# A Trainium2 decoder layer: multiplications to GpSimd, a quarter of the copies and the query casts to VectorE, value products in runs of four pairs

## The reference, cut to what matters

```
s = q k^T * scale, masked;  m = max(s);  p = exp(s - m);  o = (p v) / sum(p)
A: 6 banded heads, window 128, a learned sink per head in the maximum and the sum
B: 6 dilated heads, (window, dilation) = (128, 1), (512, 4), (2048, 16); the three
   results are combined with weights proportional to their sums
C: 4 memory heads, every token against 256 memory tokens
y = (o_A, o_B, o_C) * silu(gate)
```

## Time and profile before

| | before |
|---|---|
| median of 3 runs | 2163.92 us (2161.46 to 2164.92) |
| the profiled execution: its span | 2163.3 us |
| its own time | its span; nothing is shown around it |
| TensorE busy | 2054.7 us (95%) |
| VectorE busy | 1557.3 us (72%) |
| ScalarE busy | 1351.1 us (62%) |
| GpSimd busy | 114.9 us (5%) |
| mean granted clock of TensorE | 0.973 |

### The profile page before, as it was taken

The page is one execution under the profiler, slowest core; times in us unless marked ns, Lnnn a source line. Parts: engine busy times, 40 slices in busy tenths (PEclk is TensorE's granted clock), DMA queues, the critical chain, the costliest instruction groups (busy, mean ns, idle before and its releaser), DMA issues. The chain is left out here.

```text
span 2163.3 us, 39340 instructions
## 1 busy us (share of the span) xinstructions
PE 2054.7 (95%) x12892; PEld 1717.7 (79%) x12892; DVE 1557.3 (72%) x4410; ACT 1351.1 (62%) x3520; POOL 114.9 (5%) x116
## 2 busy tenths in 40 slices
PE   5999899999999999999899999999899998999998
PEld 4787678888888888888777887888778887788886
DVE  6564674546664574446588989989799997888887
ACT  6454454544555464343699979989689998533333
POOL 1232310000000000002000000000000000000000
PEclk7999999999999999999799989989999999999999
DMA  4477576777577657589778676686869996245543
GB/s 157 144 243 217 170 240 179 221 242 218 154 225 223 219 182 244 199 276 273 179 147 157 133 142 135 131 166 121 166 149 214 232 270 179 98 158 175 174 158 113
DMA packets 351737, 401.40 MB, mean 186 GB/s; under 512 B 105617, under 2 KB 255249, under 8 KB 346689
## 3 DMA queue, kind: packets, MB, share of 16 engines
q1 hardware_dynamic: 343120, 364.80, 61.5%
q0 software_dynamic: 8432, 34.30, 5.1%
...
## 5 line engine op out<-in xcount | busy, mean ns | idle before, releaser
L854 PE MATMUL p_ps<-p_u_hi,p_w_hi 128*128 128x512 f32 x1344 | 534.7, 398 | 25.8 <-DVE p_p_c L739 10.6
L856 PE MATMUL p_ps<-p_u_hi,p_w_lo 128*128 128x512 f32 x1344 | 526.8, 392 | 0.0
L855 PE MATMUL p_ps<-p_u_lo,p_w_hi 128*128 128x512 f32 x1344 | 526.2, 392 | 0.0
L570 DVE TENSOR_TENSOR p_w_lo<-p_w_raw,p_w_hi 128x512 fp32r<-128x512 f32 x336 | 245.7, 732 | 331.4 <-ACT p_w_hi L423 329.8
L1621 ACT ACTIVATE probs<-probs,a_stat 128x256 f32<-128x256 f32 (+1 forms) x896 | 433.7, 489 | 49.2 <-DVE a_stat L1455 45.8
L423 ACT ACTIVATE p_w_hi<-p_w_raw 128x512 fp32r<-128x512 f32 x336 | 210.7, 628 | 331.7 <-PE p_ps L856 303.7
L854 PEld LDWEIGHTS p_ps<-p_u_hi,p_w_hi 128*128 128x128 f32 x1344 | 254.1, 189 | 86.1 <-DVE p_u_lo L577 12.0
L856 PEld LDWEIGHTS p_ps<-p_u_hi,p_w_lo 128*128 128x128 f32 x1344 | 254.0, 189 | 54.5
L1455 DVE CUSTOM_DVE_ANT_0 probs<-a_ps_s,fixed 128x256 f32<-128x256 f32 (+1 forms) x704 | 251.6, 396 | 63.2 <-PE a_ps_s L1354 61.9
L855 PEld LDWEIGHTS p_ps<-p_u_lo,p_w_hi 128*128 128x128 f32 x1344 | 254.4, 189 | 50.7
L1408 PE MATMUL a_ps_o<-a_pT,a_v 128*64 128x128 f32 x3320 | 256.7, 285 | 22.8 <-ACT a_pT L1645 21.5
(11 more groups left out here) (202 smaller groups left out, 2756.5 us busy)
## 6 DMA issues: line engine op xcount, KB each, us to landing
...
p_w_raw<-scratch_w_s SPq DMA_DIRECT2D x144, 256.0 KB, 3.7
...
scratch_v<-p_out_a SPq DMA_DIRECT2D x256, 64.0 KB, 2.3
...
```

The source lines that it names most:

```text
L570: nc.vector.tensor_tensor(w_lo[:, m % 3, :, :], w_raw[:, entry(j, g), :, :], w_hi[:, m % 3, :, :].bitcast(F32), ALU.subtract).then_inc(w_l ...
L854: nc.tensor.matmul(bank, hi, u_hi[j][:, k, :], start=j < 2 and k == 0, stop=False, skip_group_check=True)
L855: nc.tensor.matmul(bank, hi, u_lo[j][:, k, :], start=False, stop=False, skip_group_check=True)
L856: last = nc.tensor.matmul(bank, lo, u_hi[j][:, k, :], start=False, stop=k == KH - 1, skip_group_check=True)
```

## The change

It does the following.

- `scale` moves from VectorE to GpSimd (`pool_parts`, `pool_round`), with the same slots. GpSimd waits for `coef_ready` at a phase's first pair and for nothing else in front of a multiplication. Its DMA loads for the output projection now follow the multiplications of certain phases (`then_load`).
- Of the copies of turned pairs, those with n % 4 == 3 (n counts pairs over all phases of a group) are made by VectorE, in the slot in which the pair is turned, after the slot's new scores. There is a semaphore for either copier.
- The four casts of a dilated phase that ScalarE did are made by VectorE, in the same slots.
- In A and C values are multiplied by runs of four pairs, in the second slot after the run's last pair; the places for copies are eight there (`NT`, `turned_place`, with four more places in a part of `probs` that these groups leave free), and the gate product follows one slot later. In B runs stay at two pairs and places at four.
- The last round has one slot more, and some semaphores that nothing used are not made.

```diff
+    NT = 4 if kind == "B" else 8
...
-    weighted, turned, turned_copied = sem("weighted"), sem("turned"), sem("turned_copied")
+    weighted, turned = sem("weighted"), sem("turned")
+    turned_copied = (sem("turned_copied_by_act"), sem("turned_copied_by_dve"))
...
+    def by_dve(n):
+        return n % 4 == 3
+    def wait_copied(eng, n):
+        if n >= 0:
+            eng.wait_ge(turned_copied[by_dve(n)], (n + 1) // 4 if by_dve(n) else n + 1 - (n + 1) // 4)
+    def place_free(eng, p, e):
+        if prev and p == 0 and (e < 4 or kind == "C"):
+            eng.wait_ge(prev.values_done, prev.TOTAL + min(e + 1 - (4 if kind == "A" else NT), 0))
+        ge(eng, values_done, p * NP + e + 1 - NT)
+    def turned_place(e):
+        if e % NT < 4:
+            return pT[:, e % NT, :, :]
+        return buf.more_pT[:, e % NT - 4, :].rearrange("p (j n) -> p j n", j=2)
 
...
-            pe.wait_ge(turned_copied, p * NP + e + 1)
+            wait_copied(pe, p * NP + e)
...
-                                            v[name][:, half, tile, :], pT[:, e % 4, j, at * P:(at + 1) * P],
+                                            v[name][:, half, tile, :], turned_place(e)[:, j, at * P:(at + 1) * P],
...
-            if prev and isinstance(p, int) and p == 0 and e < 2:
-                pe.wait_ge(prev.turned_copied, prev.TOTAL + e - 1)
-            ge(pe, turned_copied, p * NP + e - 1)
+            if prev and p == 0 and e < 2:
+                prev.wait_copied(pe, prev.TOTAL + e - 2)
+            wait_copied(pe, p * NP + e - 2)
...
-        def scale(phase, e):
-            h, s = phase
+        def copy(phase, e):
             p = number(phase)
-            if e == 0:
-                dve.wait_ge(coef_ready, p + 1 + C1)
-            for j in range(2):
-                u = FLAT[s][2 * e + j]
-                place = probs[:, s, 2 * e + j, 2 * P - u.keys:]
-                last = nc.vector.tensor_scalar(place, place, coef[:, s, u.column:u.column + 1], None, ALU.mult)
-            last.then_inc(weighted, 1)
+            if not by_dve(p * NP + e):
+                return
+            dve.wait_ge(turned, p * NP + e + 1)
+            place_free(dve, p, e)
+            a = [2 * P - FLAT[phase[1]][2 * e + j].keys for j in range(2)]
+            if a[0] == a[1]:
+                nc.vector.tensor_copy(turned_place(e)[:, :, a[0]:], ps_t[:, e % 2, :, a[0]:]).then_inc(turned_copied[1], 1)
+            else:
+                nc.vector.tensor_copy(turned_place(e)[:, 0, a[0]:], ps_t[:, e % 2, 0, a[0]:])
+                nc.vector.tensor_copy(turned_place(e)[:, 1, a[1]:], ps_t[:, e % 2, 1, a[1]:]).then_inc(turned_copied[1], 1)
 
         def copy_queries(phase, slot):
             p = number(phase)
+            if kind == "B" and slot in Q_SLOTS and p > 0:
+                i = Q_SLOTS[slot]
+                if i == 0:
+                    dve.wait_ge(scores_ready, p * NP)
+                    dve.wait_ge(q_loaded, 32 * p)
+                nc.vector.tensor_copy(q[:, 1, i * CHUNK:(i + 1) * CHUNK].rearrange("p (b i a) -> p b i a", i=4, a=8),
+                                      by_residue(q[:, 0, :])[:, 4 * i:4 * i + 4, :].rearrange(
+                                          "p i (b a) -> p b i a", a=8).bitcast(F32)).then_inc(q_copied, 1)
...
+            if by_dve(p * NP + e):
+                return
             act.wait_ge(turned, p * NP + e + 1)
-            if prev and isinstance(p, int) and p == 0 and e < 4:
-                act.wait_ge(prev.values_done, prev.TOTAL + e - 3)
-            ge(act, values_done, p * NP + e - 3)
+            place_free(act, p, e)
             a = [2 * P - FLAT[s][2 * e + j].keys for j in range(2)]
             if a[0] == a[1]:
-                nc.scalar.activation(pT[:, e % 4, :, a[0]:], ps_t[:, e % 2, :, a[0]:],
-                                     ACT.Copy).then_inc(turned_copied, 1)
+                nc.scalar.activation(turned_place(e)[:, :, a[0]:], ps_t[:, e % 2, :, a[0]:],
+                                     ACT.Copy).then_inc(turned_copied[0], 1)
             else:
-                nc.scalar.activation(pT[:, e % 4, 0, a[0]:], ps_t[:, e % 2, 0, a[0]:], ACT.Copy)
-                nc.scalar.activation(pT[:, e % 4, 1, a[1]:], ps_t[:, e % 2, 1, a[1]:],
-                                     ACT.Copy).then_inc(turned_copied, 1)
+                nc.scalar.activation(turned_place(e)[:, 0, a[0]:], ps_t[:, e % 2, 0, a[0]:], ACT.Copy)
+                nc.scalar.activation(turned_place(e)[:, 1, a[1]:], ps_t[:, e % 2, 1, a[1]:],
+                                     ACT.Copy).then_inc(turned_copied[0], 1)
...
-            p = number(phase)
-            if kind != "B" or slot not in Q_SLOTS or isinstance(p, int) and p == 0:
-                return
-            i = Q_SLOTS[slot]
-            if i == 0:
-                act.wait_ge(scores_ready, p * NP)
-                act.wait_ge(q_loaded, 32 * p)
-            by = by_residue(q[:, 0, :])
-            to = q[:, 1, i * CHUNK:(i + 1) * CHUNK].rearrange("p (b i a) -> p b i a", i=4, a=8)
-            of = by[:, 4 * i:4 * i + 4, :].rearrange("p i (b a) -> p b i a", a=8)
-            nc.scalar.activation(to, of.bitcast(F32), ACT.Copy).then_inc(q_copied, 1)
...
+            more_pT=probs[:, 0, 16:32, :].rearrange("p u n -> p (u n)").rearrange("p (k n) -> p k n", n=D)[:, :, CHUNK:],
...
-                    for i in range(n + (0 if a else 2))]
+                    for i in range(n + (0 if a else 3))]
...
-                if slot.before and slot.before[1] % 2:
+                if slot.before and slot.before[0].g.kind == "B" and slot.before[1] % 2:
                     for x, e in (slot.two_before, slot.before):
+                        x.parts.times_values(x.phase, e)
+                if slot.two_before and slot.two_before[0].g.kind != "B" and slot.two_before[1] % 4 == 3:
+                    x, last = slot.two_before
+                    for e in range(last - 3, last + 1):
                         x.parts.times_values(x.phase, e)
 
         def vector_round(a, c, b):
             for i, slot in enumerate(slots_of(a, c, b)):
                 if c and c.g.kind != "B":
                     c.parts.exchange(c.phase, i)
-                if slot.ahead:
-                    x, e = slot.ahead
-                    x.parts.scale(x.phase, e)
                 for v in slot.new:
                     a.parts.scores(a.phase, v)
+                if slot.pair:
+                    x, e = slot.pair
+                    x.parts.copy(x.phase, e)
                 if a:
                     a.parts.copy_queries(a.phase, i)
-                if slot.two_before:
+                if slot.two_before and slot.two_before[0].g.kind == "B":
                     x, e = slot.two_before
                     x.parts.finish(x.phase, e)
                 if slot.three_before:
                     x, e = slot.three_before
-                    x.parts.finish_rest(x.phase, e)
+                    if x.g.kind == "B":
+                        x.parts.finish_rest(x.phase, e)
+                    else:
+                        x.parts.finish(x.phase, e)
...
+        def pool_round(a, c, b):
+            for slot in slots_of(a, c, b):
+                if slot.ahead:
+                    x, e = slot.ahead
+                    x.parts.scale(x.phase, e)
+                    if e == x.g.NP - 1:
+                        x.parts.then_load(x.phase)
...
-                for n in range(4):
-                    pool.wait_ge(A.done_sem, (9 + n) * NC)
-                    load_sum(n)
-                for n in range(3):
-                    pool.wait_ge(C.done_sem, (1 + n) * NC)
-                    load_w(n)
+                def then_load(g):
+                    def load(phase):
+                        n = 2 * phase[0] + phase[1]
+                        if g is A and n >= 8:
+                            pool.wait_ge(A.done_sem, n * NC)
+                            load_sum(n - 8)
+                        if g is C and 2 <= n < 5:
+                            pool.wait_ge(C.done_sem, (n - 1) * NC)
+                            load_w(n - 2)
+                    return load
+                rounds(pool, pool_round, lambda g: named(scale=g.pool_parts(pool).scale, then_load=then_load(g)))
```

21 lines of the change are left out of this document (16 added, 5 removed).

## The result

The changed kernel takes 2218.91 us (median of 4 runs, 2213.38 to 2221.95) beside 2162.69 us for the kernel before in the same runs: ratio 1.0247, interval 1.0222 to 1.0271. It is slower by 2.5%. The prediction was 2109 us with a range of 2080 to 2150; the time lies outside it, on the side of the rival "GpSimd becomes the bound", which had a chance of 0.13.

The account below looks back on a forecast made before the run. TensorE was taken to bound memory and dilated heads, with all three engines full in banded ones. Banded, memory, dilated, cast, clock and tail terms totalled -54.6 us from 2163.3, giving 2109 us, range 2080 to 2150.

Parts of the forecast that it names:

- GpSimd becomes the bound: Rival, all head groups: GpSimd's multiplications outlast the phases; at 1.0 us each +88, giving 2251 us; chance 0.13.
- part 1: Attention stage: multiplications move to GpSimd at 0.40 us each, relieving VectorE of 4.7 us a banded or memory phase.
- the gains forecast for the dilated heads: Dilated heads: 4.5 of about 6.5 us of TensorE gaps vanish per head, -25 us over 5.5 heads.
- the break-even of 0.88: GpSimd's time per multiplication, near 0.88 us, at which losses and the gains kept would balance.
- the 0.2 allowed: Dilated heads: casts and gate products on VectorE each wait 0.2 us for GpSimd, 27 us over 785, off the path.
- the three falls named: Clock falls near 1262, 1430 and 1514 us, costing 18.8 us in all; half was to vanish, -9.
- Both signs by which the prediction called itself wrong: Wrong if GpSimd is busy throughout, or if a clock fall comes where none was.
- Part 2's copy: A quarter of turned-pair copies on VectorE at 0.60 us each: ScalarE -0.96, VectorE +1.2 per banded or memory phase.
- Part 3: Banded and memory heads: values in runs of four pairs save TensorE 0.68 us a phase; last copy gains a slot.
- The banded term: Banded phases fall to 12.0 us: -1.3 x 10 = -13, and -1 in the first two.
- Late copies: Rival, dilated heads: VectorE's 12 copies a head each 0.45 us late, clock falls stay; about 2137 us, chance 0.14.
- gaps 0 to 6.5 with clock 0 to 18.8: The forecast's own spread, by TensorE gaps removed per dilated head and clock loss removed: 2082 to 2137 us.

Follow-up runs that it names:

- the other form and the gate product moved: Changed kernel with GpSimd multiplying as two-tensor products (column read as stride-zero row), VectorE's copy third of four, gate product on GpSimd: 2136.38 us, ratio 0.9879.
- half-width kernel: Changed kernel, but GpSimd multiplies only half of each unit's columns, the rest left unweighted: 2136.38 us, ratio 0.9872.

## Why the prediction was wrong

**The step that failed** is in part 1: "A multiplication by a column has one tensor input, so I take 0.40", with bounds 0.31 (from the cast) and 0.64 (from the two-input addition). The term measured 0.902 us begun to begun at 256 columns, 705.5 / 764 = 0.923 with the hold-ups, and lies outside both bounds. Each bounding row was sound for its own operation: a GpSimd copy begins every 0.345 us, a product of two tensors every 0.685. What failed is the ordering put on them, that an operation with one tensor input must cost between a copy and a two-input one. On this engine the multiplication by a column is the dearest of the three.

**The rival described what happened; its chance of 0.13 was low,** for it leaned on two bounds that did not bound. Its thresholds were 0.76 us (memory), 0.83 (banded), 0.94 (dilated). At 0.902 the first two are passed: 16 x 0.902 = 14.4 us, and memory phases measured 14.4, or 15.0 to 15.2 where a load for the output projection stands among the multiplications, 14.84 on average. For the dilated heads I had counted the 21 narrow ones as half; with the fixed part they cost 80.3 / 132 = 0.608, so a head has 75 x 0.923 + 21 x 0.608 = 82.0 us of GpSimd. From the second to the twelfth coefficients a head took (1542.8 - 1133.2) / 5 = 81.9, with GpSimd busy 80.00 of 80: there too it is the bound, just. So the gains forecast for the dilated heads were used up (-4.9 us in these ten phases, and +8.0 in the first with its clock fall, instead of -25 in all), and the break-even of 0.88 was too high: the narrow ones, the hold-ups, and the seams and the end (1.3 + 2.1 + 8.2 us) were not in it.

**A term put at nothing** was that of GpSimd's own loads: "cost nothing". With GpSimd as the bound its seven loads stand in its line with no idle time around them, three of 0.811 us (L1979) and four of 0.586, 4.7 us in all.

Beside VectorE's 6.39 / 24 = 0.266 us for the same multiplication, GpSimd's 0.902 is 3.4 times. The Trainium skill (GPSIMD Engine Reference, Engine selection) advises against elementwise work on this engine. For the change as it stood the runs agree; with the other form and the gate product moved the work did pay there (0.9879). The reason that the Trainium skill gives, two inputs cost twice and one input runs at about line rate, does not fit this trace: the one-input form was the dearer.

**What held.** The reduction with one PSUM input was not held up: L1478 at 396 ns beside a full GpSimd, as before, and PSUM copies and sums the same with and without GpSimd (8.04 and 8.04). The gate product rose only from 0.687 to 0.709. The casts rose from 0.420 (all multiplications on VectorE) to 0.538, about half of the 0.2 allowed. Of the clock, half held: the three falls named went, but a fall came where none was, at 1100 to 1120 with 0.50. Both signs by which the prediction called itself wrong came true, this one and a GpSimd busy throughout.

**What would have been off even with 0.40.** The half-width kernel is the nearest test of the other parts: 2136.38, not 2109. Part 2's copy was 0.687 us at 512 elements, not 0.60. Part 3's "the last copy of four has a slot more" was wrong: the bank ring of two makes the turn after the next wait for that copy, ahead of the run of values. It cost 14 us (2136.38 to 2122.38). With that mended, memory phases are 11.80 (forecast 11.5) and dilated ones (1498.8 - 1086.1) / 11 = 37.5 (forecast 41.0 - (25 + 9) / 11 = 37.9). Banded ones are (1673.0 - 1513.7) / 11 = 14.5 with the dilated tail, against 15.1 before: -0.6 each where 14 / 11 = 1.3 was forecast. The banded term was over-sized. This kernel's window there reads:

```profile
1570.00:1690.00 120.00, 113.71 (x1151) 101.99 (x1150) 91.78 (x365) 109.35 (x372) 89.33 (x151) 0.99 0.94 233
```

Ten phases after the first took 13.0 us each. Of these ScalarE is busy 109.35 / 120 x 13.03 = 11.9, as forecast, but TensorE 12.3, not 11.7: its floor of 12.4 before, built from slots, was below its busy time (115.11 / 9 = 12.8). The phase before was also nearer 13.5 (ten took 135.1) than the 13.3 that comes of calling 144 multiplications nine whole phases.

**Two sums that do not come out.** Late copies at 12 x 0.45 a head are 5.4 x 5.5 = 30 us, of which at most the 25 forecast can go, and not 19. And gaps 0 to 6.5 with clock 0 to 18.8 give 2088 to 2143, not 2082 to 2137. Neither bears on the result.

**A part without value.** VectorE's copies bring nothing of their own. With half the columns, all copies on ScalarE and a quarter on VectorE give 2120.62 and 2122.38.
